# Gate chunks of both embedding stages on unscaled residual times the norm weight, with the root multiplied into PSUM afterwards

## What is computed

```
def rmsnorm_2(x, g):
    xf = x.astype(F32)
    y = xf * lax.rsqrt(jnp.mean(xf * xf, axis=-1, keepdims=True) + NORM_EPS)
    return (y * g.astype(F32)).astype(x.dtype)
...
        h = h + mix
        h = h + conv_glu(rmsnorm_2(h, ffn_norm[i]), ffn_w_in[i], ffn_conv_w[i], ffn_conv_b[i], ffn_w_out[i])
        e = rmsnorm_2(p[i] @ ple_w_proj[i], ple_norm[i])
        gate = jax.nn.sigmoid(rmsnorm_2(h, ple_gate_norm[i]) @ ple_w_gate[i])
        h = h + gate * e
    return rmsnorm_2(h, final_norm)
```

## Time and profile before

| | |
|---|---|
| median of 3 runs | 1279.46 us (1278.04 to 1279.78) |
| the profiled execution's own time | 1280.56 us |
| its span | 1278.4 us |
| PE busy | 1262.6 us, 99% of the span |
| DVE busy | 917.9 us, 72% |
| ACT busy | 756.3 us, 59% |
| POOL busy | 46.7 us, 4% |
| granted TensorE clock, mean | 0.996 |

### The profile page before, as it was taken

The page is one execution under the profiler, slowest core; times in us unless marked ns, Lnnn a source line. Parts: engine busy times, 40 slices in busy tenths (PEclk is TensorE's granted clock), DMA queues, the critical chain, the costliest instruction groups (busy, mean ns, idle before and its releaser), DMA issues.

```text
span 1278.4 us, 29251 instructions
## 1 busy us (share of the span) xinstructions
PE 1262.6 (99%) x12182; PEld 1231.8 (96%) x12182; DVE 917.9 (72%) x1310; ACT 756.3 (59%) x980; POOL 46.7 (4%) x38
## 2 busy tenths in 40 slices
PE   9999999999999999999999999999999999999997
PEld 8999999998899999999989999999999889999997
DVE  4779887488659887479856388665588879666557
ACT  6657665367657665368554266554466876555444
POOL 1010000010010000020000010000010001000000
PEclk9999999999999999999999999999999999999999
DMA  8464555555344555545402036555534335555520
GB/s 345 166 226 173 198 195 200 195 196 201 129 165 171 212 188 184 214 159 217 166 35 80 25 140 231 197 197 208 193 138 169 128 133 207 197 197 197 197 100 34
DMA packets 31980, 220.61 MB, mean 173 GB/s; under 512 B 3712, under 2 KB 3840, under 8 KB 6160
## 3 DMA queue, kind: packets, MB, share of 16 engines
q1 hardware_dynamic: 30672, 213.36, 45.7%
q0 software_dynamic: 784, 4.85, 1.1%
q10 hardware_dynamic: 432, 1.05, 0.2%
HBM read 218.20 MB, written 1.05 MB: 172 GB/s over the span
## 4 chain that ended last, share of the span: by engine, by line
PE 87%; DVE 8%; ACT 3%; issue 1%; POOL 0%; DMA 0%; DVEq 0%; ACTq 0%; POOLq 0%
PE ps L1913 22%; PE ps L1914 21%; PE ps L1915 21%; PE ps L1924 17%; DVE w_lo L1136 2%; PE ps L1919 2%; PE ps L1921 2%; PE ps L1920 2%; ACT w_hi L517 1%; DVE xt L1188 1%; PE ps L2138 1%; DVE xB L1199 1%; DVE xA L1199 1%; DVE xB L1160 0%; ACT L535 0%
## 5 line engine op out<-in xcount | busy, mean ns | idle before, releaser
L1136 DVE TENSOR_TENSOR w_lo<-raw,w_hi 128x2048 fp32r<-128x2048 f32 x197 | 449.5, 2288 | 135.2 <-ACT w_hi L517 134.9
L517 ACT ACTIVATE w_hi<-raw 128x2048 fp32r<-128x2048 f32 x197 | 376.3, 1915 | 157.9 <-PE ps L1915 152.5
L1913 PE MATMUL ps<-xB,w_hi 128*128 128x256 f32 x1120 | 311.4, 278 | 0.5 <-DVE w_lo L1136 0.5
L1914 PE MATMUL ps<-xB,w_hi 128*128 128x256 f32 x1120 | 309.5, 276 | 0.0
L1915 PE MATMUL ps<-xB,w_lo 128*128 128x256 f32 x1120 | 309.4, 276 | 0.0
L1913 PEld LDWEIGHTS ps<-xB,w_hi 128*128 128x128 f32 x1120 | 210.5, 188 | 2.1 <-issue 1.5
L1914 PEld LDWEIGHTS ps<-xB,w_hi 128*128 128x128 f32 x1120 | 210.5, 188 | 0.1
L1915 PEld LDWEIGHTS ps<-xB,w_lo 128*128 128x128 f32 x1120 | 210.5, 188 | 0.0
L1913 PE MATMUL ps<-xA,w_hi 128*128 128x256 f32 x744 | 208.8, 281 | 0.5 <-DVE w_lo L1136 0.5
L1915 PE MATMUL ps<-xA,w_lo 128*128 128x256 f32 x744 | 205.7, 276 | 0.0
L1914 PE MATMUL ps<-xA,w_hi 128*128 128x256 f32 x744 | 205.6, 276 | 0.0
(11 more groups left out here) (318 smaller groups left out, 1853.3 us busy)
## 6 DMA issues: line engine op xcount, KB each, us to landing
raw<-stream SPq DMA_DIRECT2D x199, 1024.0 KB, 4.8
raw<-stream SPq DMA_DIRECT2D x4, 512.0 KB, 7.9
at_bias<-rel POOLq DMA_DIRECT2D x1, 2048.0 KB, 8.3
hT<-x_t SPq DMA_DIRECT2D x4, 256.0 KB, 7.0
lora_w<-lora POOLq DMA_DIRECT2D x1, 1024.0 KB, 5.6
out_t<-xt SPq DMA_DIRECT2D x4, 256.0 KB, 2.6
hcon<-hyc POOLq DMA_DIRECT2D x1, 576.0 KB, 4.1
wsT<-wst ACTq DMA_DIRECT2D x1, 512.0 KB, 4.6
```

What stands on the lines that cost most here:

```text
L517: nc.scalar.activation(w_hi[c.slot][:], raw[c.slot][:], ACT.Copy).then_inc(hi_made, 1)
L1136: nc.vector.tensor_tensor(w_lo[c.slot][:], raw[c.slot][:], w_hi[c.slot][:].bitcast(F32), ALU.subtract).then_inc(lo_made, 1)
L1913: nc.tensor.matmul(out, wh, xh, start=start, stop=False, skip_group_check=True)
L1914: nc.tensor.matmul(out, wh, xl, start=False, stop=False, skip_group_check=True)
```

## The change

The two gate norms join `EARLY`. So `round_early` and `rest_early` make `xA` from `hT` times the weight already in the tail of the feed-forward stage before; `scale_x` and `round_x` of both stages go. The sum over partitions moves from the projection chunk into gate chunk 0 (before block 3). DVE multiplies each finished gate bank with `rs`, and ACT's sigmoid waits for that (`raw_scaled`) where it waited for PE's `chunk_used`. The banks of the gates are reordered so that bank 4, which holds the sum, is used by gate 2 only. In `gate_tail` each half is scaled by itself (128x256).

```
-GATE_BANK = (4, 6, 7, 5)
+GATE_BANK = (6, 7, 4, 5)
...
             def ple(i):
...
                square_norm(n)
-                round_x(o, xA)
...
-                        act.wait_ge(gate_half, 1)
+                        act.wait_ge(raw_scaled, SCALED_AT[n] + 4)
                         nc.scalar.activation(pl_sg[1][:, 0, :], half(5, 0), ACT.Sigmoid).then_inc(g_on, 1)
-                        act.wait_ge(chunk_used, c.count(1))
+                        act.wait_ge(raw_scaled, SCALED_AT[n] + 5)
                         nc.scalar.activation(pl_sg[1][:, 1, :], half(1, 0), ACT.Sigmoid).then_inc(g_on, 1)
...
-                    act.wait_ge(chunk_used, c.count(1))
+                    act.wait_ge(raw_scaled, SCALED_AT[n] + g + 1)
...
-            def gate_tail(n):
-
-                for b in range(2):
+            def gate_tail(n, c):
+
+                for b, out in enumerate((half(5, 0), half(1, 0))):
+                    if b:
+                        dve.wait_ge(chunk_used, c.count(1))
+                    else:
+                        dve.wait_ge(gate_half, 1)
+                    nc.vector.tensor_tensor(out, out, rs[:], ALU.mult).then_inc(raw_scaled, 1)
                     dve.wait_ge(g_on, 8 + b)
...
             def ple(i):
...
-                root(n)
-                scale_x(o, xA, f"pl_gnorm{i}")
...
                 own.wait()
+                root(n)
                 for g in range(4):
                     c = Chunk(c0 + 1 + g)
                     if g < 2:
                         split_lo(c.ahead())
...
+                    scale_early(n, g, c0 + 1 + g, GATE_BANK[g])
                     dve.wait_ge(g_on, 4 * i + g + 1)
...
             def ple(i):
...
                 for b in range(KD):
-                    if b == 4:
-                        sum_folded(n)
...
+                pe.wait_ge(h_updated, 4 * n)
                 for g in range(4):
+                    if g == 2:
+                        pe.wait_ge(rs_made, n + 1)
...
-                    early = {3: e_sums} if g == 1 else {}
-                    wide_chunk(Chunk(C0[f"pl_g{i}"] + g), GATE_BANK[g], xA, x_ready(o) if g == 0 else None, early)
+                    between = ({3: lambda: sum_folded(n)}, {3: e_sums}, {}, {})[g]
+                    wide_chunk(Chunk(C0[f"pl_g{i}"] + g), GATE_BANK[g], xA, early_ready(n) if g == 0 else None, between)
```

More of the change, by code:

```diff
@@ L72 @@
     NV += _n
-OUT_GATED, OUT_FF0, OUT_KV, OUT_Q, OUT_FF1, OUT_HY, OUT_FF2, OUT_PL0, OUT_FF3, OUT_PL1 = range(10)
+OUT_GATED, OUT_FF0, OUT_KV, OUT_Q, OUT_FF1, OUT_HY, OUT_FF2, OUT_FF3 = range(8)
 N_GM, N_FF0, N_AT, N_FF1, N_HY, N_FF2, N_PL0, N_ML, N_FF3, N_PL1, N_FIN2 = range(11)
 EARLY = {N_GM: ("a_norm", 4), N_FF0: ("f_norm0", 2), N_AT: ("kv_norm", 3), N_FF1: ("f_norm1", 2), N_HY: ("at_norm0", 3),
-         N_FF2: ("ff_norm0", 2), N_ML: ("at_norm1", 3), N_FF3: ("ff_norm1", 2)}
+         N_FF2: ("ff_norm0", 2), N_PL0: ("pl_gnorm0", 4), N_ML: ("at_norm1", 3), N_FF3: ("ff_norm1", 2),
+         N_PL1: ("pl_gnorm1", 5)}
 EARLY_AT = {n: i for i, n in enumerate(EARLY)}
@@ L87 @@
 FOLD_AT = {n: i for i, n in enumerate(FOLDED)}
-FINAL_XT = 8 * 10
-GATE_BANK = (4, 6, 7, 5)
+FINAL_XT = 8 * 8
+GATE_BANK = (6, 7, 4, 5)
 K_BANK, V_BANK, O_BANK = (3, 7, 0, 1, 2, 3, 7, 0), (1, 2, 3, 7), (0, 1, 6, 7)
@@ L983, in ple @@
             def ple(i):
-                n, o = (N_PL0, OUT_PL0) if i == 0 else (N_PL1, OUT_PL1)
+                n = N_PL1 if i else N_PL0
                 c0 = C0[f"pl_p{i}"]
                 square_norm(n)
-                round_x(o, xA)
                 for b in range(4):
@@ L1771, in ple @@
                     if i and g == 3:
-                        gate_tail(n)
+                        gate_tail(n, c)
                         break
+                    scale_early(n, g, c0 + 1 + g, GATE_BANK[g])
                     dve.wait_ge(g_on, 4 * i + g + 1)
```

## The result

| | before | after |
|---|---|---|
| median of 5 runs | 1278.31 us (1277.83 to 1279.78) | 1291.27 us (1290.35 to 1292.81) |
| profiled execution, own time | 1280.56 us | 1290.35 us |
| its span | 1278.4 us | 1288.2 us |

The changed kernel is slower: the ratio is 1.0094, 95% interval 1.0083 to 1.0105, so 10.6 to 13.4 us. The medians in the table are 13.0 us apart. The forecast was 1293.0 us. The profiled execution of the kernel before, 1280.56 us, is not one of its five runs and is longer than each of them.

The account below looks back on a forecast made before the run. PE, busy 99% of the span, was taken as the bound. Stage 0 with its successor +8.3, stage 1 +3.5 and clock +1.7 give 13.5 us, so 1293.0 us as median; range 1286.0 to 1297.5.

Parts of the forecast that it names:

- The win, -0.84 a stage: Gate chunk 0 of each embedding stage: PE's standing there goes, -0.84 us a stage.
- The cover of the moved work: Feed-forward tail before stage 0: fold ends at 934.0, PE wants its sum at 936.0; 2 us of cover, no cost.
- The alternation, +3.8: Stage 0 gates: DVE and ACT wait for each other, PE waits 4.5 us before `ml_d`, which is +3.8 against before.
- The waits in `ml_d`, 1.7, 1.65 and 2.4: Stage 0, `ml_d`: PE waits for low quarter 1, for quarter 2, and before the next norm's sum; stage total +8.3 us.
- Stage 1, +3.5: Program end: PE's sum +3.05 late, held by POOL's addition, then the last half-gate's bare scaling; +3.5 us.
- The half scaling: Last half-gate of stage 1, 128x256: its scaling lies bare on the path, 0.43 us plus a 0.04 hand-off.
- The clock, +1.7 once, uncovered: One fall of PE's clock to 1.2 GHz after the 2.4 or 3.3 us wait: +1.7 us, bounds none and 5.1.
- The sum, 13.5 us: Whole program: 8.3 + 3.5 + 1.7 = 13.5 us more, 1294.1 for the profiled execution, 1293.0 as median.
- Only its first link: Rival: alternation costs +3.8 in stage 0 only, later waits hide, no clock; 1283.5, values up to 1287; chance 0.12.
- The clock falls in every stand: Rival: PE's clock falls in every stand and stays down longer; 1298 us or more; chance 0.09.
- Not slower: Rival: win 2 x 0.84 less the bare scaling, 1278.3; chance 0.05 within 0.2%, 0.02 for a win beyond.
- The lock: POOL and DVE's shared port: each meeting could block for the whole addition, 1.74 us, two up to 1.4 more than counted.

Follow-up runs that it names:

- without the scaling: Changed kernel without the five scalings of the gates by the root and the waits for them: 1278.22 us, ratio 0.9990 to the kernel before.
- the clock was kept: Changed kernel with sixteen idle matmuls put where PE stands 4.4 us ahead of `ml_d`: 1291.22 us, ratio 1.0089 to the kernel before.
- both orders changed: Changed kernel, but DVE scales before splitting, PE sums e 30 matmuls earlier, ACT splits two gate chunks before the root: 1278.19 us, ratio 0.9989.
- stage 1 alone: Kernel before with the change in embedding stage 1 only, stage 0 the old way: 1283.37 us, ratio 1.0024.
- ACT's splits ahead: Changed kernel, but in stage 0 ACT splits the first two `ml_d` chunks one sigmoid earlier each: 1290.49 us, ratio 1.0083 to before.
- the early sums alone: Changed kernel with PE's sums of e 30 matmuls earlier and ACT splitting gate chunks before the root, DVE's order kept: 1282.73 us, ratio 1.0029.
- DVE scales first: Changed kernel, but DVE scales a gate before splitting the next chunk, then multiplies and adds: 1285.26 us, ratio 1.0042 to before.

## Why the prediction was right, and where it was off

- **The win, -0.84 a stage**: -0.82 and -0.79, measured alone without the scaling. The cover of the moved work held: the fold came 8.74 us after the first addition, as reckoned, and PE's sum in gate chunk 0 (934.72) has no wait.
- **The alternation, +3.8**: the wait for the low part of the second `ml_d` chunk was forecast at 4.5 and is 4.37, and `ml_d` starts 3.7 us late (960.75 - 923.36 against 958.28 - 924.60). DVE's gaps of 0.7 and ACT's split behind the sigmoid are in the rows. The experiments add the shares: of it 2.3 us is ACT's queue order and 2.1 DVE's, and for the whole slot the work alone is 2.6 of 8.7.
- **The waits in `ml_d`, 1.7, 1.65 and 2.4**: 0.43 and 1.69 in the profile after; 1.35, 1.36 and 1.66 where the clock was kept. The forecast counts from start to start, at 0.1133 us a matmul, and the profile's idle time only from the modelled end of the matmul before. Counted as in the forecast, the waits of the kernel with the clock kept are 965.17 - 959.80 - 32 x 0.1133 = 1.74, 968.63 - 965.17 - 16 x 0.1133 = 1.65 and 971.98 - 968.63 - 12 x 0.1133 = 1.99. So the first two were right, and then hidden in the slow clock, which the forecast had said would cost nothing there. The third was mis-sized by 0.4: I let the low part of quarter 3 run through POOL's whole second addition, and the pair took 1.39 instead of 1.9. Slot 0 was forecast at +8.3 and is +7.8, which is that 0.4 and 0.1 of the first wait.
- **Stage 1, +3.5**: +3.2. POOL's addition was taken at 2.05, as in the execution before; here it took 1.26, so the sum was held for 2.4 and not 3.05. A wait that I had not named gave 0.45 of that back: the addition for the next quarter, 1.65 beside POOL, holds that quarter's square. The half scaling is 0.42 and the hand-off 0.04, as reckoned.
- **The clock, +1.7 once, uncovered**: the term that failed for this execution. The profile after has no fall in its two slots that costs anything; the two slots give the whole of its difference. Five profiles have the stand of 2.2 us for POOL with nothing in it; in two of them it was followed by a fall, at 1.5 us in the one where it can be compared. So the price of 1.7 was near, and whether it falls due differs from execution to execution. Whether some of the unprofiled runs of the changed kernel had it is open. The profiled one is the fastest of the five although it has the fall at 65 us, and the two slowest, 1292.12 and 1292.81, have a mean granted clock of 0.992 against its 0.993; that would fit a fall in stage 1, which no trace of theirs shows.
- **The sum, 13.5 us**, against 11.0 in the slots and 13.0 (10.6 to 13.4) by the medians. 1.1 us of the forecast's distance of 1.7 is the time before, whose median over five runs is 1278.31, not 1279.46. That 13.5 lies 0.5 from the medians is in part luck: without the clock's term the forecast is 11.8, which is what the slots' 11.0 bears out, and 13.5 itself is just beyond the interval's 13.4.
- **The rivals.** "Only its first link" falls: with the first link cut to 0.95 the other three waits still stood, 4.4 us together. "The clock falls in every stand" falls too: of the stands of 4.37, 1.69 and 2.18 us in the profile after only the first brought a fall. "Not slower" was tied to one point, the low part of c0+6 at 957.5 on the axis of before. The version with both orders changed has it at 955.3 (951.76 + 2.21 - 923.31 + 924.60), by an earlier start and by giving DVE something to do while ACT works, which the forecast hadn't thought of.
- **The lock.** By the Trainium skill ("SBUF — State Buffer", section "SBUF: two separate sides") the two meetings with POOL might have cost, by my estimate, 1.4 us more than I counted. In POOL's timeline after, the two meetings in slot 0 are these:

```profile
964.11 1.28 POOL L456 TENSOR_TENSOR xt<-xt 128x512 f32<-128x512 f32 x1 [33.01 <-ACT xt L540]
970.13 1.46 POOL L460 TENSOR_TENSOR xt<-xt 128x512 f32<-128x512 f32 x1 [4.74 <-ACT xt L540]
```

The first put 1.11 us on DVE's pair of `rest_early` (1.98 against 0.87), the second 0.52 (1.39, from 970.88 on, when 0.71 of POOL's addition was left). The rule may hold, since neither is more than what was left of the addition; the 1.4 us more did not come, because the meetings were short, and the sum was 0.5 earlier than forecast.

## What to carry to other kernels

In stage 0 four extra operations of 0.69 us cost 2.6 us while nobody waited for their answer. Where an extra operation turns a one-way chain (PE to ACT to DVE) into a round trip (PE to DVE to ACT to DVE), each engine stands for the other, and whatever is queued behind the waiting instruction, here ACT's weight splits, is late with it: 0.7 us of scaling per gate became 8.7 us in a stage. Before such a change, look on the engine that sends and waits for work that fits between question and answer, and put it there; here that order alone took back 5.4 of 7.8 us in stage 0, and with DVE's row of work started earlier and the fold ahead of the last low part the change turned from 0.94% slower to 0.16% faster.

## What the runs showed of the hardware

- The same stand of PE, 2.2 us for POOL in stage 1, was followed by 2.4 GHz (granted 1.00) throughout in three profiles (the changed kernel, stage 1 alone, the clock kept ahead of `ml_d`) and by 1.2 GHz (0.50) in two (the sum's row 3.28 and 3.01 us instead of 2.34). The stand of 2.4 us at 63 us was followed by a fall in six profiles of thirteen, at 1.6 us each. One profile does not tell if a stand costs clock.
- The clock may fall late: in the run with ACT's splits ahead, PE stood 2.11 us until 959.61 and was granted 0.97 and then 0.50 in the windows from 960 and 961 on. Stands of 1.35, 1.36 and 1.69 us one after another, with work between them, brought no fall (the early sums alone); stands of 1.17 and 0.61 us brought one (DVE scales first).
- An f32 `keep_clock` matmul of 128x128 counts double in the trace (32 records for 16) and takes 0.23 us at 2.4 GHz, so sixteen are 3.73 us.
- A pair of DVE's low parts takes between 0.87 and 1.98 us, and one addition of 128x512 0.69 or 1.65, the longer ones beside an addition of POOL's.
